# First four tiles of the next dense stage made from g*x before the norm, two of them normed inside it, and the norm's lower parts moved from Pool to VectorE

## The reference

```python
for l in range(DEPTH):
    mix = _even_mixer(...) if l % 2 == 0 else _odd_mixer(...)
    h = _layernorm(DN_ALPHA * h + mix, ln_mix_g[l], ln_mix_b[l])
    f = jnp.square(jax.nn.relu(h @ mlp_w1[l])) @ mlp_w2[l]
    h = _layernorm(DN_ALPHA * h + f, ln_mlp_g[l], ln_mlp_b[l])

def _layernorm(x, g, b):
    mu = jnp.mean(x, -1, keepdims=True); xc = x - mu
    return xc * lax.rsqrt(jnp.mean(xc * xc, -1, keepdims=True) + EPS) * g + b
```

## Time and profile before

| | us |
|---|---|
| median of three runs | 3147.34 |
| lowest and highest run | 3145.82, 3153.79 |
| time of the profiled execution | 3151.24 |
| its span, first to last instruction | 3149.4 |
| TensorE matmuls busy | 2910.5 (92% of the span) |
| VectorE, ScalarE, Pool busy | 1404.2, 921.5, 607.5 |

### The profile page before, as it was taken

How to read it: one execution, slowest core, us unless ns; L and a number is a source line. 1 busy time by engine, 2 the same in 40 slices (tenths; PEclk the granted TensorE clock), 3 DMA queues, 4 the chain that set the end, 5 groups by cost and what they waited for, 6 DMA issues and landing times.

```text
span 3149.4 us, 42522 instructions
## 1 busy us (share of the span) xinstructions
PE 2910.5 (92%) x17570; PEld 2259.9 (72%) x17570; DVE 1404.2 (45%) x2488; ACT 921.5 (29%) x1715; POOL 607.5 (19%) x532
## 2 busy tenths in 40 slices
PE   8999999999999999999999898888699997998884
PEld 7659999998888778888787555555577775555552
DVE  5634323343444543233444453233588844533234
ACT  4543313232222333142322121111335721211112
POOL 1404101120111121021100352222000003522220
PEclk9999999999999999999999899999899998999997
DMA  4012222222222222222225899999622139999996
GB/s 141 26 56 68 94 94 81 94 91 66 76 81 71 67 80 94 94 94 95 80 84 214 332 414 415 417 417 415 247 81 75 48 118 364 413 415 416 415 416 264
DMA packets 239381, 600.29 MB, mean 191 GB/s; under 512 B 32647, under 2 KB 177538, under 8 KB 190026
## 3 DMA queue, kind: packets, MB, share of 16 engines
q1 hardware_dynamic: 214784, 569.47, 47.3%
q0 software_dynamic: 23904, 27.90, 2.7%
q10 hardware_dynamic: 490, 0.08, 0.0%
HBM read 607.73 MB, written 39.89 MB: 206 GB/s over the span
## 4 chain that ended last, share of the span: by engine, by line
PE 84%; DVE 5%; DMA 4%; issue 3%; ACT 2%; POOL 1%; SPq 0%; ACTq 0%; DVEq 0%; POOLq 0%
PE ps L101 79%; PE ps L104 5%; DMA sb_arena<-in_exp_w_dram 2%; DVE sb_tmpA L118 1%; DMA sb_wx<-in_exp_w_dram 1%; DVE sb_arena L126 1%; DVE sb_arena L118 1%; DVE sb_ws L118 1%; SPq L144 0%; POOL sb_arena L118 0%; DMA sb_arena<-y_rows 0%; DVE sb_tmpA L129 0%; ACT sb_arena L112 0%; DMA sb_arena<-x_rows,sb_smallu 0%; ACT sb_hs L108 0%
## 5 line engine op out<-in xcount | busy, mean ns | idle before, releaser
L101 PE MATMUL ps<-sb_hs,sb_ws 128*128 128x264 f32 (+1 forms) x6384 | 1106.6, 335 | 17.3 <-ACT sb_hs L108 7.5
L101 PEld LDWEIGHTS ps<-sb_hs,sb_ws 128*128 128x128 f32 x6384 | 971.2, 190 | 148.1 <-issue 16.5
L118 DVE TENSOR_TENSOR sb_ws<-sb_ring,sb_ws 128x1024 fp32r<-128x1024 f32 x279 | 370.5, 1333 | 425.7 <-ACT sb_ws L112 425.2
L112 ACT CAST sb_ws<-sb_ring 128x1024 fp32r<-128x1024 f32 x279 | 290.7, 1046 | 333.6 <-PE ps L101 318.1
L101 PE MATMUL ps<-sb_arena 128*64 128x256 f32 (+18 forms) x1652 | 351.9, 426 | 28.7 <-issue 21.9
L101 PE MATMUL ps<-sb_br,sb_ws 128*128 128x264 f32 (+1 forms) x2304 | 367.4, 322 | 0.0
L101 PEld LDWEIGHTS ps<-sb_br,sb_ws 128*128 128x128 f32 x2304 | 332.4, 188 | 34.1 <-issue 0.5
L101 PE MATMUL ps<-sb_ring,sb_arena 128*64 128x256 f32 (+2 forms) x1506 | 274.1, 435 | 27.3 <-issue 24.5
L101 PEld LDWEIGHTS ps<-sb_arena 128*64 128x64 f32 (+6 forms) x1652 | 200.5, 162 | 132.2 <-issue 74.4
L108 ACT ACTIVATE sb_arena<-ps 64x256 f32<-64x256 f32 (+6 forms) x192 | 76.0, 407 | 747.2 <-PE ps L101 722.8
L118 DVE TENSOR_TENSOR sb_arena<-sb_arena,ps 64x256 f32<-64x256 f32 (+1 forms) x160 | 66.4, 423 | 494.9 <-ACT sb_arena L108 454.8
(11 more groups left out here) (198 smaller groups left out, 2599.9 us busy)
## 6 DMA issues: line engine op xcount, KB each, us to landing
sb_ring<-in_exp_w_dram SPq DMA_DIRECT2D x113, 1024.0 KB, 27.8
sb_hx<-in_exp_w_dram SPq DMA_DIRECT2D x92, 1024.0 KB, 28.2
sb_arena<-in_exp_w_dram SPq DMA_DIRECT2D x66, 1024.0 KB, 28.3
sb_wx<-in_exp_w_dram SPq DMA_DIRECT2D x66, 1024.0 KB, 28.1
sb_ring<-in_mlp_w_dram SPq DMA_DIRECT2D x64, 1024.0 KB, 5.1
sb_hT<-in_exp_w_dram SPq DMA_DIRECT2D x47, 1024.0 KB, 28.6
sb_ring<-in_od_w_in_dram SPq DMA_DIRECT2D x24, 1024.0 KB, 5.3
sb_ring<-in_conv_w_in_dram SPq DMA_DIRECT2D x12, 1024.0 KB, 5.0
```

The source lines that it names most:

```text
L101: return self.e.matmul(o, l, r, start=start, stop=stop, skip_group_check=True)
L112: return self.e.copy(o, i)
L118: return self.e.tensor_tensor(o, a, b, op)
```

## The change

1. In the stage ahead of each norm ScalarE writes the upper part of g*x for each of the 8 tiles (`raw_act`) and VectorE the lower part (`raw_dve`), into free space of `arena` under the name `raw`, with g and b as two more columns. In the two MLPs the space is free only when half of the last tiles' inputs have been read, so six of the eight are written at once at tile 6 there.
2. The next stage's first four tiles (two columns of 256 features) are made from `raw`. The statistics and the root's broadcast stand inside the first pair, at steps 2 and 4 (`ln_hooks`). Halves have half the tokens each, the second with two columns more.
3. These four tiles are normed afterwards: ScalarE copies the two extra columns out (`normed_vectors_act`), VectorE does two operations (`normed_dve`), ScalarE one (`normed_act`). Tiles 0 and 1 are normed inside `ln_act` and `ln_dve` (`finish`), tiles 2 and 3 behind the norm.
4. ScalarE copies mean and root out of PSUM. The norm's lower parts are made by VectorE (`lower`); Pool has no `ln_pool`. The eight in-place results in `hT` are made after all upper parts.
5. The weight splits for tiles 2, 3 and 4 stand inside the norm, those for tiles 0 and 1 of the stage behind it are left out.
6. `ln_first_pe` of norm 2 moves into the last output tile, as in the others.

```diff
+        def split_raw(u, T):
+            return [(u[:, 0:T // 2], 0, T // 2), (u[:, 512:514 + T // 2], T // 2, T + 2)]
...
-                        if k == 4 and between is not None:
-                            between()
+                        if k in between:
+                            between[k]()
...
             x, T = of_norm(hT[:, m, :], l), span(l)[1]
             e.wait_ge(*summed[stage, m])
+            if l > 0:
+                e.wait_ge(*act_ln["y", l - 1, m])
...
+        RAW_LATE = {0: (), 1: (7,), 2: (5, 6, 7), 3: (7,)}
...
+        def raw_x(l, first=0):
+            T = span(l)[1]
+            return lambda k: (raw_of(l, 0, k)[:, first:T + 2], raw_of(l, 1, k)[:, first:T + 2], x_hi["raw", l, k],
+                              x_lo["raw", l, k])
...
+        def raw_act(e, l, m):
+            T, (g, c) = span(l)[1], LNW[l]
+            ks = raw_group(l, m)
+            if m == 0 and l in half_read:
+                e.wait_ge(*summed["part", half_read[l]])
+            e.wait_ge(*dve_emptied[LNSTAGE[l], m])
+            if ks:
+                o, v = raw_vectors(l, 0, ks)
+                e.acp(o, v).then_inc(*x_hi.mark(("raw vectors", l, ks[0])))
+            e.act(raw_of(l, 0, m)[:, 0:T], of_norm(hT[:, m, :], l), ACT.Identity, scale=vec(g + "_g", 8 * c + m)).then_inc(
+                *x_hi.mark(("raw", l, m)))
+        def raw_dve(e, l, m):
+            T, (g, c) = span(l)[1], LNW[l]
+            ks = raw_group(l, m)
+            e.wait_ge(*x_hi["raw", l, m])
+            if ks:
+                o, v = raw_vectors(l, 1, ks)
+                e.tt(o, v, raw_vectors(l, 0, ks)[0].bitcast(F), ALU.subtract).then_inc(
+                    *x_lo.mark(("raw vectors", l, ks[0])))
+            e.stt(raw_of(l, 1, m)[:, 0:T], of_norm(hT[:, m, :], l), vec(g + "_g", 8 * c + m),
+                  raw_of(l, 0, m)[:, 0:T].bitcast(F), ALU.mult, ALU.subtract).then_inc(*x_lo.mark(("raw", l, m)))
...
+        def normed_vectors_act(e, key, at, T):
+            e.wait_ge(*summed[key])
+            e.acp(sm[:, 20 + 2 * at:22 + 2 * at], U_[key][:, 512 + T // 2:514 + T // 2]).then_inc(*act_ln.mark(("gb", key)))
+        def normed_dve(e, l, key, at, o, T):
+            first = span(l)[1] - T
+            mean, rs = (x[:, first:first + T] for x in mean_rows(l))
+            e.wait_ge(*act_ln["gb", key])
+            e.wait_ge(*summed[key])
+            e.wait_ge(*act_emptied["mean", l])
+            e.stt(halves(o), halves(mean), raw_vector_of(at)[0], halves(U_[key])[:, :, 0:T // 2], ALU.mult,
+                  ALU.subtract).then_inc(*dve_ln.mark(("less", key)))
+            e.wait_ge(*dve_ln["less", key])
+            e.wait_ge(*act_emptied["rs", l])
+            e.tt(o, o, rs, ALU.mult).then_inc(*dve_ln.mark(("z", key)))
+        def normed_act(e, key, at, o, fn, signal, mark):
+            e.wait_ge(*dve_ln["z", key])
+            e.act(o, o, fn, scale=-1.0, bias=raw_vector_of(at)[1]).then_inc(*signal.mark(mark))
...
+        def ln_hooks(e, units, l):
+            return {2: lambda: ln_stats_pe(e, l), 4: lambda: ln_root_pe(e, units.take(e, ("rs", l)), l)}
+        def ln_act(e, l, finish):
             g, i = LNW[l]
+            T = span(l)[1]
+            split_hi(e)
             e.wait_ge(*dve_ln["inv", l])
             n = len(span(l)[2])
             e.act(sm[:, 75:75 + n], sm[:, 70:70 + n], ACT.Sqrt).then_inc(*act_ln.mark(("rs", l)))
+            for x, what in zip(mean_rows(l), ("mean", "rs")):
+                e.wait_ge(*normed[what, l])
+                e.wait_ge(*dve_emptied["stat", l])
+                e.acp(fit(x, T), whole(U_[what, l], T)).then_inc(*act_emptied.mark((what, l)))
+            def upper(ms):
+                for m in ms:
+                    x, b = of_norm(hT[:, m, :], l), vec(g + "_b", 8 * i + m)
+                    e.wait_ge(*dve_ln["scaled", l, m])
+                    e.act(of_norm(HS[:, 0, m, :], l), x, ACT.Identity, bias=b).then_inc(*x_hi.mark(("ln", l, m)))
+            upper(range(3))
+            split_hi(e)
+            finish(0)
+            finish(1)
+            upper(range(3, 6))
+            split_hi(e)
+            upper(range(6, 8))
             for m in range(8):
                 x, b = of_norm(hT[:, m, :], l), vec(g + "_b", 8 * i + m)
-                e.wait_ge(*dve_emptied["scaled", l, m])
-                e.act(of_norm(HS[:, 0, m, :], l), x, ACT.Identity, bias=b).then_inc(*x_hi.mark(("ln", l, m)))
-                e.wait_ge(*x_hi["ln", l, m])
+                e.wait_ge(*x_lo["ln", l, m])
                 e.act(x, x, ACT.Identity, bias=b).then_inc(*act_ln.mark(("y", l, m)))
...
             def less(m):
                 x = of_norm(hT[:, m, :], l)
-                e.wait_ge(*normed["mean", l])
-                e.tt(fit(x, T), fit(x, T), whole(U_["mean", l], T), ALU.subtract).then_inc(
-                    *dve_emptied.mark(("less", l, m), *([("mean", l)] if m == 7 else [])))
-
-            less(0)
-            for m in range(8):
+                e.wait_ge(*act_emptied["mean", l])
+                e.tt(x, x, mean, ALU.subtract).then_inc(*dve_ln.mark(("less", l, m)))
+            def scaled(m):
                 x = of_norm(hT[:, m, :], l)
-                if m < 7:
-                    less(m + 1)
-                e.wait_ge(*dve_emptied["less", l, m])
-                e.wait_ge(*normed["rs", l])
-                e.stt(fit(x, T), fit(x, T), vec(g + "_g", 8 * c + m), whole(U_["rs", l], T), ALU.mult,
-                      ALU.mult).then_inc(*dve_emptied.mark(("scaled", l, m), *([("rs", l)] if m == 7 else [])))
-
-        def ln_pool(e, l):
-            for m in range(8):
-                e.wait_ge(*act_ln["y", l, m])
-                e.tt(of_norm(HS[:, 1, m, :], l), of_norm(hT[:, m, :], l), of_norm(HS[:, 0, m, :], l).bitcast(F),
-                     ALU.subtract).then_inc(*x_lo_pool.mark(("ln", l, m)))
+                e.wait_ge(*dve_ln["less", l, m])
+                e.wait_ge(*act_emptied["rs", l])
+                e.stt(x, x, vec(g + "_g", 8 * c + m), root, ALU.mult, ALU.mult).then_inc(*dve_ln.mark(("scaled", l, m)))
+            def lower(m):
+                e.wait_ge(*x_hi["ln", l, m])
+                e.stt(of_norm(HS[:, 1, m, :], l), of_norm(hT[:, m, :], l), vec(g + "_b", 8 * c + m),
+                      of_norm(HS[:, 0, m, :], l).bitcast(F), ALU.add, ALU.subtract).then_inc(*x_lo.mark(("ln", l, m)))
+            split_lo(e)
+            for m in range(4):
+                less(m)
+            scaled(0)
+            scaled(1)
+            lower(0)
+            scaled(2)
+            lower(1)
+            lower(2)
+            finish(0)
+            finish(1)
+            split_lo(e)
+            scaled(3)
+            less(4)
+            scaled(4)
+            lower(3)
+            less(5)
+            scaled(5)
+            lower(4)
+            split_lo(e)
+            lower(5)
+            less(6)
+            scaled(6)
+            less(7)
+            scaled(7)
+            lower(6)
+            lower(7)
...
-                dense_all(e, ("w1", l), [(2048 * hf + 256 * i, 256) for i in range(8)], 8, ln_x(2 * l), T, units)
+                cols = [(2048 * hf + 256 * i, 256) for i in range(8)]
+                if hf == 0:
+                    dense_all(e, ("w1", l), cols[:2], 8, raw_x(2 * l), T, units, True, ln_hooks(e, units, 2 * l), raw=True)
+                    cols = cols[2:]
+                dense_all(e, ("w1", l), cols, 8, ln_x(2 * l), T, units, hf > 0)
...
+        def first_act(e, l, m):
+            key, T = (("w1", l), m), span(2 * l)[1]
+            normed_vectors_act(e, key, m, T)
+            normed_act(e, key, m, (MU, RS)[m % 2][:, 0:T], ACT.Relu, act_emptied, key)
+        def first_dve(e, l, m):
+            T = span(2 * l)[1]
+            if m >= 2:
+                e.wait_ge(*x_lo["ff", l, 0, m - 2])
+            normed_dve(e, 2 * l, (("w1", l), m), m, (MU, RS)[m % 2][:, 0:T], T)
...
-                    split_hi(e)
-                    e.wait_ge(*summed[("w1", l), m])
-                    if m >= 2:
+                    if 2 <= m < 31:
+                        split_hi(e)
+                    if m in (2, 3):
+                        first_act(e, l, m)
+                    if m >= 4:
+                        e.wait_ge(*summed[("w1", l), m])
                         e.wait_ge(*x_lo["ff", l, (m - 2) // 16, (m - 2) % 16])
-                    e.act(fit(x, T), whole(U_[("w1", l), m], T), ACT.Relu).then_inc(*act_emptied.mark((("w1", l), m)))
+                        e.act(fit(x, T), whole(U_[("w1", l), m], T), ACT.Relu).then_inc(
+                            *act_emptied.mark((("w1", l), m)))
...
                     out_splits(e, split_hi, m)
+                    if hf and m == 6:
+                        for k in range(6):
+                            raw_act(e, 2 * l + 1, k)
                     if hf:
                         square_act(e, ("w2", l, 1), m, 2 * l + 1)
-            ln_act(e, 2 * l + 1)
+                    if hf and m >= 6:
```

(32 more changed lines are left out.)

197 lines of the change are left out of this document (131 added, 66 removed).

## The result

The changed kernel takes 3167.89 us (median of four runs, 3164.66 to 3171.17), the kernel before in the same session 3146.61 (3145.82 to 3153.79): ratio 1.0059, 95% interval 1.0046 to 1.0072: slower by 0.6%, which the interval keeps clear of no change. The profiled execution took 3171.17 us, with a span of 3169.0 against 3149.4. The forecast was 3161 in a range of 3148 to 3174: the sign is right, the size 7 us too small.

What follows compares the result with a forecast made beforehand. The chain of waits is mostly matmul lines, so only what moves TensorE's instructions counts. 3.3 + 6.7 + 1.5 + 2.5 = 14.0 us on the profiled 3151.24 gave 3165, with the median 3.9 lower 3161; range 3148 to 3174.

Steps and rivals of the forecast that it cites:

- E: Mark at each norm: the end of the last output tile's matmuls; the forecast counted its times from there.
- So far the change is 5.6 us ahead of now: First norm, at tile 4: its weights ready at E+29.4 after a 1.1 us wait, tile 4 done at E+35.3.
- terms for norm 1: Norm before the retention: tile 7 starts 6.2 us later behind the rotation, plus 0.7 for the clock after the second wait.
- the low clock of the earlier trace: Kernel before: where TensorE idled 4.32 us before 1713.65, the clock was 0.50 until about 1718.6, five us after restart.
- Pool's squares: Relu squares inside the norm: each could hold VectorE up for 1.07, 2 us a norm; taken as 0.
- hand-overs between VectorE and ScalarE: Bound for the first norm: each of some 30 hand-overs between engines 0.05 longer gives +4.8 instead of +3.3.
- No wait at tile 5: Rival: tile 5's cast is done before TensorE ends tile 4; -15, 3132 us; chance 0.07.
- A quicker chain with the clock kept: Rival: no clock loss and VectorE's operations 10% shorter with SBUF inputs; +4.6, 3152 us; chance 0.26.
- E delayed by work ahead of it and by Pool's squares: Rival: 3 us in two norms from work ahead of E, and Pool's squares in the way; 3171 us; chance 0.15.
- The wait at each tile 5: Sign: TensorE waits 5.5 to 7 us for a lower weight half, four times, some 35 us behind each E.
- No wait above 1.5: Sign: ahead of the wait at tile 5, no TensorE wait longer than 1.5 us.
- the second wait in the retention: Sign: at the norm before the retention, TensorE waits again, about 4 us, for tile 7's weights behind the rotation.

Runs made afterwards that it cites:

- e1: Changed kernel with ScalarE's eight in-place results of each norm made one by one behind later tiles' casts, not in a row ahead of tile 5's cast: 3145.48 us.
- e7: Changed kernel with the lower weights of tiles 7 and 8 split inside the rotation at norm 1, not behind it: 3162.04 us.
- e8: e5 with two 512-column f32 filler matmuls ahead of tile 4 at norms 0 and 2: 3137.98 us.
- e2: Changed kernel with only the split of tile 5's weights moved ahead of the eight in-place results, on both engines: 3165.17 us.
- e4: Changed kernel with Pool making the norms' lower parts again and each in-place result right behind its upper part; raw tiles stay: 3156.63 us.
- e6: e5 with tile 4's weights also split right behind tile 3's, on both engines: 3140.10 us.
- e3: Changed kernel with five 512-column f32 filler matmuls on TensorE while it waits for tile 5's weights, in each of four norms: 3167.57 us.
- e5: Changed kernel with the changes of e1 and e7 together: 3139.65 us, ratio 0.9968 to the kernel before.

## Why the prediction was right, and where its sum was short

**The mechanism held.** The forecast put a new wait for a lower weight half at tile 5, behind the eight in-place results, four times. Measured starts of tile 5 behind E, with the forecast in brackets: 43.0 (42.1), 40.6 (40.7), 41.2 (39.8), 39.3 (38.7). Tiles 0 and 1 end at E+16.1 (16.1), tile 3 starts at 22.4 (22.35), the eight last 5.10 (5.2), and at norm 1 tile 7 starts at 58.0 (58.6) behind 3.98 us of waiting (4.1). e1 shows that the eight operations cause the wait, e7 that the rotation causes the second one.

**Tile 4.** "So far the change is 5.6 us ahead of now" was too much. Tile 4's weights came at E+30.4, not 29.4; 0.8 of that is the scaling that lasts 1.57 beside Pool's square, a cost that the forecast had weighed and set at nothing. And tile 4 ran in part at 0.50 behind 1.79 us of waiting, which the forecast didn't foresee at all. It was done at E+38.1, 2.8 us earlier than before and not 5.6. So tile 5's wait was 4.90, not 6.8: TensorE came later to it, its weights only 0.9 later. By e7 and e8 the slow tile itself costs nothing here; only the 0.9 is lost.

**The sum.** 14.0 was forecast for the four norms, 20.7 measured (6.2 + 7.6 + 3.4 + 3.5), and 0.9 was gained ahead of them, which is within the scatter of that stretch.

| norm | forecast | measured | what was mis-sized |
|---|---|---|---|
| 0 | +3.3 | +6.2 | tile 5's weights 0.9 later; 1.8 at low clock just ahead of norm 1's E |
| 1 | +6.7 | +7.6 | until tile 7's start +5.6, forecast 6.2; behind it +2.0, forecast 0.7 for the clock |
| 2 | +1.5 | +3.4 | tile 5's weights 1.4 later |
| 3 | +2.5 | +3.5 | tile 5's weights 0.6 later |

The forecast's own terms for norm 1, 6.2 and 0.7, make 6.9, but its sum has 6.7; and it read the low clock of the earlier trace rows to last until 1718.6, where the mean of 0.68 over 1718 to 1720 says about 1719.3. Neither matters to the result. Of the 6.7 us that are missing in all, 2.9 are weights that came later than counted at norms 0, 2 and 3. The forecast set Pool's squares at nothing, and they account for 1.6 of the 2.9: at norms 0 and 2, the two with squares, a scaling lasts 1.57 and 1.52 beside one, and 0.77 and 0.75 without. The other 1.3 would fit hand-overs between VectorE and ScalarE that were counted too tight, for which the forecast had a bound of 0.05 us each (+1.5 a norm); they were not measured one by one. 0.9 are norm 1's, 1.8 us are a stretch that the forecast never looked at, and 1.1 were not resolved. That stretch is the last matmuls ahead of norm 1:
```profile
673.40 1.92 PE L101 MATMUL ps<-sb_tmpA,sb_cst 128*128 128x264 f32 x4
674.74 2.85 PE L101 MATMUL ps<-sb_br,sb_ws 128*128 128x264 f32 x12
```
The same instructions take 1.14 and 1.83 in the kernel before, so 0.78 and 1.02 are lost; the granted clock here is 0.65 from 673 to 675 and 0.50 from 675 to 677. The twenty small matmuls of the statistics, 2.29 us, stand just ahead of them in both. The same stretch is slow in e2, e4, e6, e7 and e8 and at full clock in the kernel before, e1, e3, e5; in e4 the matching stretch ahead of norm 0 is slow too (12 matmuls in 3.21 us), and in no other. So the 1.8 us may be chance and not the change; that was not settled.

**The rivals.** No wait at tile 5: refuted. A quicker chain with the clock kept: refuted on both counts, the weights came later at three of the four norms and the clock fell to 0.50. E delayed by work ahead of it and by Pool's squares: E itself was not delayed at norm 0 (it came 0.9 sooner), no wait stands ahead of E at the others, and nothing waited for Pool's sums; but its second half, Pool's squares in VectorE's way, was there, at 0.8 us at norms 0 and 2. The time of 3168 is nearer to the 3171 which that rival gave than to the forecast's 3161, for other reasons in the main.

**The signs.** Three of the signs named in advance were not met as stated. The wait at each tile 5 was to be 5.5 to 7 us and was 4.90, 5.39, 6.49 and 5.46. No wait above 1.5 was to stand ahead of it, and 1.79 and 1.83 do, at norms 0 and 2. Tile 4 was to be done 5 us earlier and was 2.8 earlier at norm 0. The rest held: a clock of 0.50 behind all four waits, and the second wait in the retention.
